# Gate and up weights of the experts split into two fp32r halves, and a new order of loads between two layers

## What is computed

```python
for l in range(DEPTH):                      # 2 layers
    h = rms_norm(x, norm1_gain[l])
    z = h @ w_in[l]                         # 1024 x 2048: q, k, v, u
    ...                                     # attention, pooling
    x = x + concat([att, pool]) @ w_out[l]
    t = rms_norm(x, norm2_gain[l])
    gates = ...                             # top 1 of 4 groups, then top 2 of its 4 experts, 16 in all
    hg = einsum('td,edf->tef', t, w_gate[l])    # expert: 1024 -> 256
    hu = einsum('td,edf->tef', t, w_up[l])
    a = silu(hg) * hu * gates[..., None]
    x = x + einsum('tef,efd->td', a, w_down[l])  # 256 -> 1024
```

## Time and profile before

| | |
|---|---|
| time of the runs, us | 1723.99 median of 3 (1722.34 to 1726.35) |
| profiled execution, us | 1723.27, its span 1721.4 |
| PE busy, us | 1491.7 (87%) |
| DVE, ACT, POOL busy, us | 781.1 (45%), 452.3 (26%), 315.3 (18%) |
| chain that ended last | PE 77%, DVE 7%, issue 6%, DMA 3% |
| of it L1566 and L1579 | 19% and 9% |
| HBM read, written | 170.77 MB, 49.28 MB |

### The profile page before, as it was taken

How to read it: one execution, slowest core, us unless ns; L and a number is a source line. 1 busy time by engine, 2 the same in 40 slices (tenths; PEclk the granted TensorE clock), 3 DMA queues, 4 the chain that set the end, 5 groups by cost and what they waited for, 6 DMA issues and landing times.

```text
span 1721.4 us, 22556 instructions
## 1 busy us (share of the span) xinstructions
PE 1491.7 (87%) x6963; PEld 1079.8 (63%) x6964; DVE 781.1 (45%) x1883; ACT 452.3 (26%) x886; POOL 315.3 (18%) x204
## 2 busy tenths in 40 slices
PE   5999978998992999999289998899999749999990
PEld 4878867886882444444178786788778624444440
DVE  5777656663336122212267866656533452212210
ACT  4231245662111011111222222567412101111110
POOL 1000068001000122222500001930200012222224
PEclk9999989999995999999599999899999869999995
DMA  8000020000168499973870002000002945999947
GB/s 314 19 1 0 0 98 1 2 1 1 73 222 291 156 283 298 341 223 89 226 222 0 1 0 98 1 1 2 1 25 90 330 154 160 270 301 280 311 91 162
DMA packets 116624, 221.09 MB, mean 128 GB/s; under 512 B 5976, under 2 KB 72736, under 8 KB 116544
## 3 DMA queue, kind: packets, MB, share of 16 engines
q1 hardware_dynamic: 91744, 131.82, 22.2%
q0 software_dynamic: 19136, 69.38, 16.4%
q10 hardware_dynamic: 5664, 18.88, 2.8%
HBM read 170.77 MB, written 49.28 MB: 128 GB/s over the span
## 4 chain that ended last, share of the span: by engine, by line
PE 77%; DVE 7%; issue 6%; DMA 3%; ACT 2%; POOL 1%; ACTq 1%; DVEq 0%; PEld 0%; PEldq 0%; POOLq 0%; SPq 0%
PE ps L1566 19%; PE ps L1360 17%; PE ps L1340 11%; PE ps L1493 9%; PE ps L1579 9%; PE ps L1446 7%; PE ps L1420 2%; DMA out_x<-x_res,arena 2%; PE ps L1507 2%; PE ps L1422 1%; POOL out_x L622 1%; DVE arena L1149 1%; PE ps L1480 1%; DVE w_in_lo L944 1%; DMA big<-in_w_in 1%
## 5 line engine op out<-in xcount | busy, mean ns | idle before, releaser
L1566 PE MATMUL ps<-big,arena 128*128 x720 | 325.8, 606 | 9.6 <-issue 8.3
L1340 PE MATMUL ps<-cst,arena 128*128 128x128 f32 x1242 | 186.4, 284 | 76.4 <-DVE arena L915 37.6
L905 DVE TENSOR_TENSOR arena<-ps,par 128x512 f32<-128x512 f32 x126 | 81.2, 686 | 355.8 <-PE ps L1340 355.8
L1566 PEld LDWEIGHTS ps<-big,arena 128*128 128x128 f32 x720 | 135.7, 194 | 170.4 <-issue 170.4
L1340 PEld LDWEIGHTS ps<-cst,arena 128*128 128x128 f32 x1242 | 152.6, 146 | 122.7 <-DVE arena L915 39.3
L1360 PE MATMUL ps<-w_in_hi,hT_hi 128*128 128x512 f32 x512 | 206.1, 402 | 12.7 <-DVE hT_lo L933 9.9
L1360 PE MATMUL ps<-w_in_hi,hT_lo 128*128 128x512 f32 x512 | 202.1, 395 | 0.0
L1360 PE MATMUL ps<-w_in_lo,hT_hi 128*128 128x512 f32 x512 | 201.9, 394 | 0.0
L614 POOL DMA_INDIRECT x_res<-token_rows,row_tok x62 | 61.0, 985 | 605.1 <-issue 309.2
L1579 PE MATMUL ps<-big,arena 128*128 x360 | 163.8, 598 | 5.4 <-issue 5.4
L1446 PE MATMUL ps<-big,arena 128*128 128x64 f32 x1152 | 149.7, 278 | 0.0
(11 more groups left out here) (169 smaller groups left out, 1770.1 us busy)
## 6 DMA issues: line engine op xcount, KB each, us to landing
big<-in_w_gate SPq DMA_DIRECT2D x32, 1024.0 KB, 10.6
big<-in_w_up SPq DMA_DIRECT2D x32, 1024.0 KB, 13.1
big<-in_w_down SPq DMA_DIRECT2D x32, 1024.0 KB, 15.3
big<-in_w_in SPq DMA_DIRECT2D x16, 1024.0 KB, 9.5
big<-in_w_out SPq DMA_DIRECT2D x4, 2048.0 KB, 10.3
token_rows<-arena ACTq DMA_DIRECT2D x16, 512.0 KB, 3.3
out_x<-x_res ACTq DMA_DIRECT2D x16, 512.0 KB, 4.1
x_res<-out_x SPq DMA_DIRECT2D x8, 512.0 KB, 5.8
```

What stands on the lines that cost most here:

```text
L905: ins = ve.tensor_tensor(out=dst[:, 4 * h:4 * h + 4, :], in0=ps[:, banks + h, :].rearrange("p (a c) -> p a c", c=P), in1=spread(gain[:, 4 ...
L1340: ins = te.transpose(ps[:, bank + i // 4, (i % 4) * P:(i % 4 + 1) * P], src, ident)
L1566: ins = te.matmul(ps[:, 2, :], xgT[:, k, :], big[:, ds(at + k * 2 * FE, 2 * FE)], start=k == 0, stop=k == K - 1)
```

## The change

- **Experts' gate and up.** For each half (512 of the 1024 input numbers) of each block's gate and up weights ACT makes a high half (`gu_high`) and DVE a low half (`gu_low`), into three buffers; half n = 2t + h goes to buffer n mod 3. The turned rows are split too: `rows_high` on ACT, the subtraction in `rows_evac` on DVE, into the place of x tiles 0 and 1. `gate_up` becomes 24 fp32r products. It reports its first half (`gu_half`), which frees a buffer. The expert's number is read into a register for each half, on ACT and DVE.
- **Order.** ACT in block t: high half (t+1, 1), silu, rows of t+1, high half (t+2, 0), y of t-1, aT. DVE: low half (t+1, 1), act, rows of t+1, low half (t+2, 0), y of t-1. The list of gates on PE moves behind `gate_up(0)`.
- **Loads.** Gate/up and down of an expert have semaphores of their own; gate/up is loaded once expert e-4 is split. Input number 8p + k, not 128k + p, now lies on partition p, so a partition's gate or up weights are one piece of 8 KB. The gain of the norm is loaded as a row and multiplied into `xs2`. Padding rows are gathered no more (index beyond the bound).
- **Next layer.** The first quarter of `w_in` goes into the slot of expert 12, behind its last down product, and is split when all blocks are over. SP loads x tiles 0 and 1 first, directly behind the last used scatter, and only then steps `spare_may`, for which ACT waits before it reports spare blocks; then the second quarter, tiles 2 to 4 behind the gathers, tiles 5 to 7 behind all scatters, `wpool` last.

```diff
-                    sp.wait_ge(dn_done, upto(l, BLOCKS, used - BLOCKS))
-                    load_in(l, 1, 2)
...
+                    sp.wait_ge(s_add, upto_added(0, used))
                     sp.sem_inc(s_passed, 1)
                     for t in range(2):
                         sp.dma_start(xr[:, t, :], out[t * P:(t + 1) * P, :]).then_inc(s_again[t], 16)
+                    sp.sem_inc(spare_may, 1)
+                    sp.wait_ge(dn_done, upto(l, BLOCKS, used - BLOCKS))
+                    sp.wait_ge(gu_split, upto(l, 2 * BLOCKS, 0))
+                    load_in(l, 1, 2)
...
+                for e in range(SLOTS, NE + 2):
+                    if e < NE:
+
+                        ended = sp.value_load(start_i[0:1, e - SLOTS + 1:e - SLOTS + 2], min_val=0, max_val=BLOCKS)
+                        sp.wait_ge(gu_split, upto(l, 2 * BLOCKS, 2 * ended))
+                        sp.sem_inc(s_passed, 1)
+                        load_gu(e)
+                    if SLOTS < e <= NE:
+                        report_gu(e - 1)
+                    d = e - 2
+                    if d >= SLOTS:
+                        ended = sp.value_load(start_i[0:1, d - SLOTS + 1:d - SLOTS + 2], min_val=0, max_val=BLOCKS)
                         sp.wait_ge(dn_done, upto(l, BLOCKS, ended))
...
+                def gu_high(t, slot, h, half_of=None):
+
+                    e = a_.value_load(block_e[0:1, ds(t, 1)], min_val=0, max_val=NE - 1)
+                    if half_of is not None:
+                        a_.wait_ge(gu_half, upto(l, BLOCKS, half_of + 1))
+                        a_.sem_inc(s_passed, 1)
+                    a_.wait_ge(gu_loaded, upto(l, NE, e + 1))
+                    a_.sem_inc(s_passed, 1)
+                    at = ((e + 2) % SLOTS) * E_ALL + AT_E
+                    sc.activation(gu_hi[(2 * slot + h) % 3].rearrange("p (g c) -> p g c", g=2), raw_gu(at, h),
+                                  ACT.Copy).then_inc(gu_top, 1)
...
                 def moe_act(t, slot, m):
+                    if not last(t, BLOCKS):
+                        gu_high(t + 1, (slot + 1) % RING, 1, t)
                     a_.wait_ge(gu_done, upto(l, BLOCKS, t + 1))
                     sc.activation(sg, ps[:, 2, 0:FE], ACT.Silu).then_inc(silu_done, 1)
+                    if not last(t, BLOCKS):
+                        a_.wait_ge(xgT_ready, upto(l, BLOCKS, t + 1))
+                        rows_high(t + 1)
+                    if not near_end(t, BLOCKS):
+                        gu_high(t + 2, (slot + 2) % RING, 0)
                     if not first(t):
                         moe_down(t - 1, *before(slot, m))
...
-                        a_.wait_ge(s_add, upto_added(l, t + 1))
-                        a_.sem_inc(x_whole, 1)
                     with a_.Else():
+                        a_.wait_ge(spare_may, upto(l, 1, 1))
...
+                def gu_low(t, slot, h):
+
+                    dve.wait_ge(gu_top, upto(l, 2 * BLOCKS, 2 * t + h + 1))
+                    dve.sem_inc(s_passed, 1)
+                    e = dve.value_load(block_e[0:1, ds(t, 1)], min_val=0, max_val=NE - 1)
...
                 def moe_dve(t, slot, m):
                     if not last(t, BLOCKS):
-                        rows_evac(t + 1)
+                        gu_low(t + 1, (slot + 1) % RING, 1)
                     dve.wait_ge(silu_done, upto(l, BLOCKS, t + 1))
                     ve.scalar_tensor_tensor(out=act, in0=ps[:, 2, FE:2 * FE], scalar=list_gate[:, ds(t, 1)], in1=sg,
                                             op0=ALU.mult, op1=ALU.mult).then_inc(a_ready, 1)
+                    if not last(t, BLOCKS):
+                        rows_evac(t + 1)
+                    if not near_end(t, BLOCKS):
+                        gu_low(t + 2, (slot + 2) % RING, 0)
                     if not first(t):
                         y_evac(t - 1, *before(slot, m))
...
                 with dve.If(l < DEPTH - 1):
+                    in_low(l + 1, 0, [0])
                     norm_x(l + 1, 0, 0)
+                    in_low(l + 1, 0, [1])
                     dve.wait_ge(gain_in, upto(l + 1, 1, 1))
...
-                def gate_up(t):
-                    at = weights(t)
+                def gate_up(t, slot):
                     for k in range(K):
-                        ins = te.matmul(ps[:, 2, :], xgT[:, k, :], big[:, ds(at + k * 2 * FE, 2 * FE)],
-                                        start=k == 0, stop=k == K - 1)
+                        h = k // (K // 2)
+                        if k % (K // 2) == 0:
+                            pe.wait_ge(gu_split, upto(l, 2 * BLOCKS, 2 * t + h + 1))
+                        c = slice(k % (K // 2) * FE, (k % (K // 2) + 1) * FE)
+                        hi, lo = (w[(2 * slot + h) % 3].rearrange("p (g c) -> p g c", g=2)[:, :, c] for w in (gu_hi, gu_lo))
+                        for n, (a, b) in enumerate(((xgT_hi, hi), (xgT_hi, lo), (xgT_lo, hi))):
+                            ins = te.matmul(ps[:, 2, :].rearrange("p (g f) -> p g f", g=2), a[:, k, :], b, start=k == 0 and n == 0,
+                                            stop=k == K - 1 and n == 2)
+                        if k == K // 2 - 1:
+                            ins.then_inc(gu_half, 1)
```

More of the change, by code:

```diff
@@ L477, in _ @@
                 load_in(l, 2, 1)
+                sp.wait_ge(win_split, upto(l, 8, 2))
                 load_in(l, 3, 3)
@@ L1595, in moe_pe @@
                     pe.sem_inc(s_passed, 1)
-                    gate_up(t)
+                    gate_up(t, slot)
+                    if first(t):
+                        list_gates()
                     if not last(t, BLOCKS):
```

209 lines of the change are left out of this document (142 added, 67 removed).

## The result

The changed kernel takes 1751.99 us (median; 1745.54 to 1754.39) against 1724.39 for the kernel before: ratio 1.0154, 95% interval 1.0125 to 1.0184. The forecast was 1703 us, with a range of 1672 to 1728 and a chance of 0.11 for slower, so the time lies outside the range. The profiled execution took 1754.39 us, its span is 1752.6, 31.2 longer than before.

A forecast was written before the change was run, and what follows sets the result against it. PE was taken to bound the expert stage before, an ACT-DVE loop after. Expert stage -16.2, its start +5.3, between layers -5.6, end -6, small ones +1.4: -21.1 us, giving 1703 us, range 1672 to 1728.

The forecast's parts named there:

- Bound, and what the split saves: Expert stage: bound by PE's columns; three fp32r products cut gate/up from 6.96 to 5.47 us, 1.49 less a block.
- PE stays the bound: Rival, expert stage: register overhead hidden or small, a block takes 10.1 us, 1656 us in all; chance 10 in 100.
- The loop: Expert blocks: ACT and DVE wait for each other in turn, 11.2 us a block including 1.15 us overhead per exposed register load.
- the loop is as long as PE's turn now: Rival, expert stage: overhead of 1.45 us a load gives 11.8 us a block, 1723 us in all; chance 15 in 100.
- Folding the gain: Projection: gain multiplied into xs2, beside PE for seven tiles, bare on the last; 0.5 us more a layer.
- The last block: End of each layer's expert stage: the last gate/up is not in a loop, 2 x 1.4 = 2.8 us less.
- Start of the stage: From expert numbers to first gate/up: splits have no cover, 2.6 us later in each layer, 5.3 for both.
- Between the layers: From last down product into layer 2: z 1.0 us sooner and the 4.58 us stop at tile 2 gone, 5.6 us less.
- Less traffic: Expert loads: gathers of padding rows now move nothing; no gain booked under loads.
- The end: Behind the last scatter that counts: ACT's wait for its landing and four spare gathers go, 6 us less.
- POOL is locked: Rival, expert stage: two-input DVE splits hold up POOL's scatter, 12.1 us a block, 1735 us in all; chance 8 in 100.
- Weights come late: Rival, expert stage: eight waits of 3 us where experts have one block each, 1727 us; chance 5 in 100.

The follow-up runs named there:

- The run in plain order: The changed kernel with xs2 written in plain order by the multiply and the transposes reading every eighth column: 1736.51 us, ratio 1.0065.
- the kernel with all the edits together: The changed kernel with plain multiply, VectorE's early register load and early half of y, and ScalarE's single load: 1666.24 us, ratio 0.9662.

## Why the forecast was wrong, point by point

**Bound, and what the split saves: right.** Gate/up takes 5.47 to 5.48 us, and PE's own turn is the 10.0 us that was worked out. (The rival "PE stays the bound" takes 39 x 1.2 off; from 11.2 to its 10.1 it is 39 x 1.1, so 1660 and not 1656 us.)

**The loop: right in form, its overhead mis-sized.** By the 14 sure blocks of layer 1, in the means, with the forecast behind each: aT to the copy 1.39 (1.15), the copy and the hand-over 3.28 (1.90 + 1.15), remainder, activation and rows 3.95 (4.00, less most of the 0.25 for seams), second remainder 2.20 (2.29), y and hand-over 0.92 (0.92): 11.73 against 11.16. The failed step is "I estimate 1.15 us" for what goes with a register load: it was 1.39 and 1.36. With a short load it is less than the estimate, 1.01 to 1.05 on ACT and from 0.95 on DVE. What lifts the mean are the long loads, and on ACT the turn of the loop in every third block (1.49 to 1.57). I had taken the 0.32 to 0.55 of the earlier trace rows, which were read ahead of the first scatter of their layer; half of the loads inside a scatter's flight are long. The rival "the loop is as long as PE's turn now" had put 1.45 and 11.8 us: it, and not the forecast, described the sure block. Its 1723 fell short by the terms below and by 5.6 us in the blocks under the If, where the two hand-overs were longer still: 1.97 and 1.71 us in layer 1. In sum: +14.4 us for 28 blocks and +9.4 for 11 under the If (12.59 and 12.26 instead of 11.5), 23.8 of the 52 us between -21.1 and +31.2, the largest miss. This miss alone would have left the time at 1727 us, just inside the range; folding the gain and the last block took it out.

One thing neither the forecast nor its rivals had is TensorE's clock. Before, each of the 28 sure blocks ran at a granted clock of 1.00. After, six of the 39 gate/up products took 7.3 to 7.4 us in place of 5.7, each with a mean granted clock of 0.77 (part of it at the lower level, 1.2 GHz), behind 2.0 to 2.7 us in which PE did only the two transposes. That is 10 us of TensorE's time at most; how much of it reached the loop is not separated from the rest.

**Folding the gain: 16.4 us, the largest miss outside the loop.** The step that failed is "a two-input 128x1024, whose row is 1.23 ... beside PE for seven tiles, bare on the last". I priced the operation by its shape and did not look at its access pattern, which stands in the diff; it took 2129 ns and not 1225. And I named PE as its cover without measuring it. A tile of the projection went from 107.7 / 8 = 13.5 to 114.6 / 8 = 14.3 us (first to last product of layer 1), so the cover was used up in each tile. The run in plain order shows both parts.

**The last block: 10.1 us, of the wrong sign.** I wrote "not in a loop, 2 x 1.4 = 2.8" less. But ACT and DVE, in the last real block, still copy and subtract one half of the weights of each of two blocks that don't exist, and aT waits behind them. Timeline after, end of layer 1:

```profile
834.45 2.28 DVE L1359 TENSOR_TENSOR gu_lo<-big,gu_hi 128x2048 fp32r<-128x2048 f32 x1
836.64 0.68 DVE L1389 COPY x_res<-ps 128x512 f32<-128x512 f32 x1
837.58 0.38 ACT L929 ACTIVATE arena<-ps 128x256 f32<-128x256 f32 x1 [3.89 <-DVE x_res L1389]
...
839.36 6.24 PE L1711 MATMUL ps<-big,arena 128*128 x8 [5.46 <-issue]
```

The subtraction at 834.45 is for no block. PE has been idle for 5.46 us when the last down product begins, and then takes 6.24 us for what took 3.60 at 829.13. Its granted clock was 0.59, at the lower level (1.2 GHz) until 844.5. The page gives the granted clock in 40 slices of 43.8 us, in tenths; the twentieth, 832 to 876 us, is at 5:

```profile
PEclk9999989999995899999599999899999859999995
```

Before, the same product took 5.39 us at 0.68, behind 2.69 us of idleness. So of the 10.1 us one part is the longer wait and one the clock after it. In the kernel with all the edits together, y ahead of that subtraction and one load on ACT among them, the stretch is 16.7 us in both layers, where the forecast had asked for 18.3 and 16.7.

**Start of the stage: right** (+4.7 for +5.3; the 558.8 in its working should be 558.5 by its own prices); the first two blocks cost 1.8 more, where I had booked nothing.

**Between the layers: near in size (-4.1 for -5.6), wrong in its cause.** I had put it to the order of loads; the order alone gives +4.0 there, and with the skipping gathers -3.1. "Less traffic", which I had booked at nothing, was the term that carried it in these two executions. Both parts of the forecast failed: z did not start sooner at all (31.5 us behind the last down product, 31.6 before), and the stop did not go, it fell from 4.58 to 2.23 us. The last scatter that counts lands in 6.13 us for 11.33, as forecast. The gain is not firm: with the plain multiply it is gone (67.0 us, 64.6 before).

**The end: right** (-7.4 for -6); the order alone gives 4.6 and with the gathers 8.1.

**POOL is locked:** gathers do take longer beside the two-input subtractions (2.68 us at 652.51 for 1.04 at 830.26), but the rival's path, aT behind the scatter's landing, is not what ended the waits: the wait of aT is put down to y, 155.6 us, 43 times. It showed only when the loop had been opened, as the 34.4 us above do. **Weights come late:** no wait for a load of expert weights is among the large ones of any kernel here.

## What to carry to other kernels

When work moves from the engine that is the bound to two others that are each half idle, add up the loop through both, with every register load, check and semaphore in it, by the mean of such a load and not by its shortest case, and look at what is queued ahead of the hand-over: here one copy moved by one place and one load moved ahead of one wait were worth 38 and 50 us in a kernel that the change itself made 28 us slower. Price an operation by its access pattern and not by its shape alone. And a block loop that prepares ahead prepares for blocks that don't exist: look at what the last real one waits for.

## What the hardware showed that I had not expected

- A register load from SBUF takes 0.27 to 0.31 us on VectorE and ScalarE, but 0.6 to 1.3 us in half of the cases inside the flight of an adding scatter (51 of 103), and only in 6 and 4 of 98 when the scatter does not add. TensorE's loads (0.30, at most 0.38 in that kernel) were never long. In the kernel with the load early on VectorE, y ahead and the plain multiply none of VectorE's 96 was long (at most 565 ns), though 46 of them started inside a flight, while on ScalarE 20 of 41 still were; what in the flight does it is open.
- A 128x1024 two-input fp32 operation on VectorE takes 1285 ns with contiguous inputs and 2129 ns when both are read with a step of eight elements; TensorE's weight loads of such columns take 188 ns in place of 140, which stays hidden beside transposes of 273.
- An indirect transfer whose indices are all out of bounds takes GpSimd 1.04 us (gather) and 1.55 to 1.60 us (scatter) all the same, but frees the transfer engines: with skipping scatters 188.77 MB in place of 204.42 in the whole kernel, and 17 to 22 us.
- The same 2.74 us of idleness before the same down product was followed by a granted clock of 1.00 in one kernel (3.70 us) and of 0.54 in another (6.75 us), the gate/up and transposes before it being the same. Two profiles can differ by 3 us for that alone.
